# The odd-slot v sums of tile 1 made on GpSimd beside VectorE: a one-core Trainium2 kernel of two transformer blocks

## The reference, cut to what matters

```
u_e = u[experts]                      # per token 128 rows of 1024
v_e = v[experts]                      # per token 128 rows of 1024
a = gelu(einsum('td,thkd->thk', xb, u_e))
out = einsum('thk,thkd->td', g * a, v_e)
```

## Time and profile before

| | |
|---|---|
| median of 3 runs | 1665.5 us (1662.28 to 1666.78) |
| the profiled execution's own time | 1661.12 us |
| its span in the trace | 1659.3 us |
| PE / DVE / ACT / POOL busy | 1353.2 / 921.1 / 485.2 / 286.6 us |
| moved by the transfers | 511.99 MB, mean 309 GB/s |

### The profile page before, as it was taken

One profiled execution on the slowest core, in us unless ns is written; L12 is line 12 of the kernel. 1 busy time (PEld: TensorE's weight loads), 2 busy tenths in 40 slices (PEclk: granted clock), 3 DMA queues, 4 the chain that ended last, 5 costly groups with the idle time before them and its releaser, 6 DMA issues.

```text
span 1659.3 us, 17926 instructions
## 1 busy us (share of the span) xinstructions
PE 1353.2 (82%) x6236; PEld 954.3 (58%) x6236; DVE 921.1 (56%) x1877; ACT 485.2 (29%) x1177; POOL 286.6 (17%) x294
## 2 busy tenths in 40 slices
PE   7999988998777838666885768777569998988996
PEld 3887655653223318566674535545268977756772
DVE  4875348577799646699848875454522641421001
ACT  2103313333323333444426613111322231422112
POOL 0120003344434512222202131112000000000000
PEclk9998998999999979977956679999879995999998
DMA  9990129999999979999977799999848563247883
GB/s 365 339 333 26 51 102 401 421 421 422 421 421 421 422 304 409 422 394 372 422 308 281 276 378 392 422 420 422 358 157 287 181 238 115 80 152 251 298 299 136
DMA packets 71988, 511.99 MB, mean 309 GB/s; under 512 B 8144, under 2 KB 8288, under 8 KB 10976
## 3 DMA queue, kind: packets, MB, share of 16 engines
q0 software_dynamic: 40400, 290.46, 43.3%
q1 hardware_dynamic: 30496, 216.77, 34.8%
q10 hardware_dynamic: 1008, 3.67, 0.6%
HBM read 509.81 MB, written 1.05 MB: 308 GB/s over the span
## 4 chain that ended last, share of the span: by engine, by line
PE 54%; DMA 22%; DVE 12%; issue 7%; ACT 4%; POOL 1%; SPq 0%; DVEq 0%; POOLq 0%; ACTq 0%
DMA arena<-in_experts,arena 11%; DMA ring<-in_weights 11%; PE bank L948 9%; PE bank L978 6%; PE bank L958 6%; PE bank L923 5%; PE bank L1014 4%; PE bank L878 3%; PE bank L1112 3%; PE bank L707 3%; PE bank L695 3%; PE bank L723 2%; DVE junk L1852 1%; DVE junk L1863 1%; DVE junk L1846 1%
## 5 line engine op out<-in xcount | busy, mean ns | idle before, releaser
L923 PE MATMUL bank<-arena,diag 128*128 128x512 f32 x512 | 240.2, 619 | 59.9 <-ACT diag L1359 59.9
L948 PEld LDWEIGHTS bank<-act_t,ring 128*128 128x128 f32 x2048 | 245.4, 200 | 46.6 <-issue 40.1
L948 PE MATMUL bank<-act_t,ring 128*128 128x128 f32 x2048 | 249.6, 283 | 26.7 <-DMA ring<-in_weights 20.7
L1852 DVE SCALAR_TENSOR_TENSOR junk<-arena,bank 128x1024 f32<-128x1024 f32 x128 | 155.6, 1216 | 117.3 <-DMA arena<-in_experts,arena 117.0
L629 POOL DMA_INDIRECT arena<-in_experts,arena x128 | 132.6, 1036 | 473.9 <-DVE junk L1863 436.1
L923 PEld LDWEIGHTS bank<-arena,diag 128*128 128x128 f32 x512 | 96.9, 196 | 195.4 <-issue 110.8
L1846 DVE SCALAR_TENSOR_TENSOR junk<-arena,bank 128x1024 f32<-128x1024 f32 x128 | 153.9, 1219 | 65.3 <-DMA arena<-in_experts,arena 61.9
L605 POOL DMA_INDIRECT arena<-in_experts,arena x128 | 127.5, 996 | 322.9 <-PE bank L923 175.9
L1863 DVE SCALAR_TENSOR_TENSOR junk<-arena,junk 128x1024 f32<-128x1024 f32 x127 | 162.5, 1280 | 8.1 <-ACT arena L1379 7.6
L958 PE MATMUL bank<-ring,act_t 128*128 128x256 f32 x576 | 132.1, 388 | 10.7 <-DMA ring<-in_weights 10.7
L1233 ACT ACTIVATE arena<-bank 128x512 f32<-128x512 f32 x74 | 43.6, 597 | 309.3 <-PE bank L958 86.8
(11 more groups left out here) (270 smaller groups left out, 1841.6 us busy)
## 6 DMA issues: line engine op xcount, KB each, us to landing
ring<-in_weights SPq DMA_DIRECT2D x201, 1024.0 KB, 5.8
arena<-in_ada_weights POOLq DMA_DIRECT2D x16, 1024.0 KB, 7.2
arena<-in_experts,arena POOLq DMA_INDIRECT x256, 14.4
row<-in_rows_in ACTq DMA_DIRECT2D x7, 512.0 KB, 3.8
arena<-in_ada_weights SPq DMA_DIRECT2D x2, 1024.0 KB, 11.3
arena<-in_rpb POOLq DMA_DIRECT2D x4, 512.0 KB, 12.9
res<-in_x SPq DMA_DIRECT2D x1, 1024.0 KB, 11.5
arena<-in_ctx_in SPq DMA_DIRECT2D x1, 1024.0 KB, 13.2
```

The lines of the kernel that those rows point to most:

```text
L923: last = mm(bank(j), diag[:, k % 4, :], bufs[k % N_BUF][:, D + half * 512:D + half * 512 + 512], start=(k == 0), stop=(k == SLOTS - 1))
L948: last = mm(b[:, at + m * P:at + m * P + P], w[:, c, m * P:m * P + P], act_t[:, c, t * P:t * P + P], start=(c == 0), stop=(c == C - 1))
L1852: v.scalar_tensor_tensor(junk[:, 0, :], bufs1[k % N_BUF1][:, 0:D], 1.0, x_nat_at(1), ALU.mult, ALU.mult, accum_out=dots[:, 1, k:k + 1]).th ...
```

## The change

DVE keeps the v sums of the even slots. Those of the odd slots go to POOL, into an accumulator of their own, `summed_odd`, which lies in the v half of a buffer that tile 0 has done with. Instead of one fused instruction, POOL has two: for each odd slot it scales the gathered v in place (tensor_scalar) and adds it to the accumulator (tensor_tensor), with a wait on its own semaphore `odd_scaled` between. Slot 1 is written by the scaling alone. POOL does this in its one queue, four slots behind the gathers. At the end DVE adds the two accumulators in one more tensor_tensor.

```diff
+        summed_odd = arena[:, BUF_AT + 5 * UNIT - D:BUF_AT + 5 * UNIT]
...
+        ODD_LAG = 4
...
+            def odd_value(k):
+
+                value, by = bufs1[k % N_BUF1][:, D:2 * D], factors[:, 1, k:k + 1]
+                pool.wait_ge(factor_ready, SLOTS + k + 1)
+                if k == 1:
+                    pool.wait_ge(freed[4], len(range(4, SLOTS, N_BUF)))
+                    last = nc.gpsimd.tensor_scalar(summed_odd, value, by, None, ALU.mult)
+                else:
+                    nc.gpsimd.tensor_scalar(value, value, by, None, ALU.mult).then_inc(odd_scaled, 1)
+                    pool.wait_ge(odd_scaled, k // 2)
+                    pool.wait_ge(freed1[(k - 2) % N_BUF1], (k - 2) // N_BUF1 + 1)
+                    last = nc.gpsimd.tensor_tensor(summed_odd, summed_odd, value, ALU.add)
+                last.then_inc(freed1[k % N_BUF1], 1)
...
             for k in range(SLOTS):
...
                     bounds_check=N_EXPERTS - 1, oob_is_err=False).then_inc(gathered1[k % N_BUF1], 16)
+                if k >= ODD_LAG and (k - ODD_LAG) % 2:
+                    odd_value(k - ODD_LAG)
+            for k in range(SLOTS - ODD_LAG, SLOTS):
+                if k % 2:
+                    odd_value(k)
...
-                    dve.wait_ge(freed1[(k - 1) % N_BUF1], (k - 1) // N_BUF1 + 1)
+                    dve.wait_ge(freed1[(k - 2) % N_BUF1], (k - 2) // N_BUF1 + 1)
...
-                    if g:
+                    if g and k % 2 == 0:
                         second_value(k - GROUP)
...
-                    for k in range(SLOTS - GROUP, SLOTS):
-                        second_value(k)
-                    dve.wait_ge(freed1[(SLOTS - 1) % N_BUF1], len(range((SLOTS - 1) % N_BUF1, SLOTS, N_BUF1)))
+                    second_value(SLOTS - 2)
+                    for k in range(SLOTS - 2, SLOTS):
+                        dve.wait_ge(freed1[k % N_BUF1], len(range(k % N_BUF1, SLOTS, N_BUF1)))
...
+                    link(v.tensor_tensor(summed, summed, summed_odd, ALU.add))
```

More of the change, by code:

```diff
@@ L332, in build @@
         own_of = [Own(t) for t in range(TT)]
-        assert own_of[0].end <= OWN[1] and own_of[1].end <= ARENA, (own_of[0].end, own_of[1].end)
+        assert own_of[0].end <= OWN[1] - D and own_of[1].end <= ARENA, (own_of[0].end, own_of[1].end)
         banks = stack.enter_context(nc.psum_tensor("bank", [P, 8 * 512], F32))
@@ L390, in build @@
         ya_ready = sem("ya_ready")
+        odd_scaled = sem("odd_scaled")
         rot_ready = sem("rot_ready")
```

## The result

| | before | after |
|---|---|---|
| median | 1666.1 us (1662.3 to 1666.9, 4 runs) | 1695.2 us (1691.5 to 1698.4, 4 runs) |
| ratio, 95% interval | | 1.0179 [1.0154, 1.0205] |
| the profiled execution's span | 1659.3 us | 1692.5 us |

The changed kernel is 1.8% slower, some 29 us; the two profiled spans are 33 us apart. The prediction had the sign and the range (1682, 1660 to 1712); its sum of 17 us was little more than half of the 29.

The account below looks back on a forecast made before the run. From 697 to 840 us DVE's order was taken as the bound, transfers right behind. Terms 4 + 2.5 + 7 + 2 - 1 + 2.5 = 17 us on 1661.1 gave 1678, set on the median 1682; range 1660 to 1712 us.

Parts of the forecast that it names:

- heavier: Whole kernel: slow scalings or waiting dots bring the time to 1695 to 1725 us; chance 0.17.
- the exemption: Tile 1's dots, one SBUF and one PSUM input, never wait for POOL and stay at 1.21 us.
- The full-load stretches: Where gathers and weights fill the transfers, a pair has about 10 us, POOL needs 6.8: nothing gained or lost.
- The faster rival: Whole kernel: POOL's port lock hardly meets DVE, so the time falls by 5 us to 1660 us; chance 0.15.
- The mis-sized term: the scaling: POOL's scaling of 128x1024 per pair, taken as 1.2 us between bounds of 1.0 and 2.2 us.
- with only the scaling at 2.2 us ... about 1700: POOL's round of 7.8 us exceeds DVE's 7.4, pairs lose 0.5 to 1 us more; within the 0.17 case.
- the levels: Twelve pairs, 710 to 796 us: round of three pairs grows from 22.1 to 23.0 us, +4 us in all.
- the burst behind the heads: Shares at 955 to 970 us: later gathers cost +2 us; a v sum before 984 us gives -1 us.
- At the end: After the last dot, POOL's last scaling and addition and DVE's joining addition delay the gate product by 2.5 us.
- The attention: One share per two heads: +1.0 us a pair for 7 pairs, +7 us in all.
- The lock: DVE instructions with two SBUF inputs stand still until POOL's tensor_tensor has ended; extended to POOL's scaling.
- The three pairs ahead of 830 us: Three pairs between 796 and 833 us, ahead of two-input products: +0.8 us each, +2.5 us in all.

Follow-up runs that it names:

- the levels alone: Kernel before, with ACT scaling and POOL adding odd slots beside the dots only in shares 12 to 23: 1663.75 us, ratio 0.9981.
- levels and heads: Kernel before, with ACT scaling and POOL adding odd slots beside the dots in shares 12 to 23 and 29 to 37: 1662.29 us, ratio 0.9993.
- nothing: Changed kernel with the odd v sums left out of the result, POOL only marking odd buffers free: 1648.96 us, ratio 0.9913 against before.
- queue with writes: Changed kernel with POOL's scaling and addition replaced by five memsets per odd slot, odd sums left out: 1669.99 us, ratio 1.0036 against before.
- queue with reads: The changed kernel itself, POOL scaling and adding the odd slots: 1695.2 us, ratio 1.0179 against before.

## Why the prediction was right, and what of its sum was not

**Right in kind, short in size.** 1695.2 us lies in the range of 1660 to 1712, but just past the band "as forecast (1671 to 1695)", in the one called heavier, to which I gave 0.17: the sign is shown, the size was covered by a wide range and not by the sum. DVE's busy time did not fall, single two-input instructions of 2 to 3 us stand among normal ones, additions take 2.35 us (2.2 in the sum), dots 1.215 us: the exemption that I had only one weak row for the earlier trace rows holds for all 128 of them. The full-load stretches are worth nothing either way, shown by the run that moved 18 pairs there. The faster rival is excluded; its ceiling was higher than I thought (14 us where I had 5), but it needs a POOL that does nothing.

**The mis-sized term: the scaling.** "I take 1.2 us, near the memset" should have been 2.86 us. It was the term without a row; both ends of my bounds, 1.0 and 2.2, lay below the truth, since I took the two-input instruction for the upper one. The run in which ACT scales shows what the term was worth: by the two ratios some 13 us of the loss go with it. The Trainium skill, "GPSIMD Engine Reference", section 3.1, would give an estimate of 0.9 us, and the measurement contradicts it by a factor of three. With 2.86 for 1.2 POOL's round is 6.8 + 1.7 = 8.5 us (8.2 measured) and longer than DVE's; so the rival "with only the scaling at 2.2 us ... about 1700" is nearer to what happened in the levels (+7.8 for +4) and in the burst behind the heads (+5.0 for +1), and the outcome, 1695, lies between forecast and rival. At the end it took 3.75 us, of which 1.4 show (+3.9 for +2.5), since it began beside DVE's last v sum and not behind it.

**The attention** cost 9.1 us for 7, but not only by the steps I named. The scaling was to end just behind the second head's L2133 (L2156 in after) and harm nothing, and the addition was to fall on tensor_scalars or v sum. In the trace both harm: in one kind of pair L2156 takes 1.73 us and the two tensor_scalars 1.83, in the other the second tensor_scalar takes 1.97 us, all by the scaling, and the v sum of 908.98 took 2.32 us beside the addition.

**The lock.** "A DVE instruction with two SBUF inputs stands still until POOL's tensor_tensor has ended" was right to 0.2 us. Extended to the scaling it was wrong both ways: two-input forms wait until about 1 us into it and no longer, and tensor_scalars, which I had not counted among those that wait for it, stay out until its end when they come after that. The rule of the Trainium skill, "SBUF — State Buffer", "Who interferes with whom", a lock for the whole instruction, fits the addition (let in 2.15 of 2.35 us into it); for two-input forms beside the scaling (0.93 of 2.86 us) the measurement contradicts it.

**What gave back.** The three pairs ahead of 830 us cost 3.0 us (2.5 in the sum), and 3.0 us were gone again behind DVE's wait for PE: the wait was 22.4 us long in before and 20.8 in after, and the shares just ahead of it, which have two v sums less, took 1.4 us less. I had counted the 2.5 us through to the end.

**What is open.** 3.9 us stand at 697 us already. Of these 2.2 stand at 600 us, ahead of the first instruction that was changed: scatter of single executions. The other 1.7 us can be scatter too, for the runs with the levels alone and with levels and heads are the same program up to 697 us, and are 3.7 and 0.3 us late at that mark; it isn't shown. The 2.3 us between 1172 and 1194 us no run explains. How the loss divides between port and queue is known only roughly: nothing, queue with writes, and queue with reads give 0.9913, 1.0036 and 1.0179, so some 20 us for the queue (and what memsets do to DVE's one-input forms) and 24 us for the reads, less the 14 us of work saved. By the traces, counted from 600 to 1208 us, it is 16 and 25 us, less 11. The two are not independent, since a DVE that waits also frees its buffers later. Why the scaling lets two-input instructions in after a microsecond, keeps later tensor_scalars out, and is felt ahead of its listed start isn't settled.

## What to carry to other kernels

Before work goes to an idle engine, price three things: its own duration from a run on that engine (never from a neighbour's time per input), what else stands in that engine's queue (here all gathers), and which of the first engine's forms share its port. An engine that is 17% busy on average, and a quarter in the stage that mattered, was the fullest of that stage with the work on it. Ask first what the work is worth where it stands, by a run that leaves it out: here 14 us of 82.

A share of transfers of 1.00 is not yet the ceiling: read the GB/s beside it against the best stretch of the same kernel.

## What the runs showed of the hardware that was not expected

- POOL's tensor_scalar with one input is slower than its tensor_tensor with two: 2.86 against 2.35 us for 128x1024 f32 (medians of 63 each); and its tensor_tensor with the same tensor as both inputs took 1.90 us.
- DVE instructions with one SBUF and one PSUM input of 1024 elements (the dots of tile 1) ran at 1214 to 1218 ns on the mean in every one of these kernels, whatever POOL did; the longest took 1223 ns.
- DVE's tensor_scalar from SBUF to SBUF waits for POOL's memsets too (608 ns where 286), two-input instructions don't (v sums 1280).
- After an addition of POOL the next gather's issue starts 0.15 us later, but some gathers' issues last 1.3 to 2.0 us where 1.0 is usual, in the kernel before too.
